# Conditioned decoder layer, one core: modulation two channel blocks ahead, first weight block earlier in two queues, remainders first in each VectorE step

## What is computed

```python
c_act = jax.nn.silu(c)
mod = (c_act @ w_ada[l] + b_ada[l])[:, None, :]
sh1, sc1, g1, sh2, sc2, g2 = jnp.split(mod, N_MOD, axis=-1)
h = rmsnorm(x, norm1_g[l]) * (1 + sc1) + sh1
z = h @ w_in                      # then split into u, gb, gc, v, ga, gg
...                               # pooling, short conv, Conformer conv -> y
x = x + g1 * y
h = rmsnorm(x, norm2_g[l]) * (1 + sc2) + sh2
x = x + g2 * (jnp.square(jax.nn.relu(h @ w_ff1[l])) @ w_ff2[l])
```

## Time and profile before

| | us |
|---|---|
| median of 3 runs | 1137.24 (1134.82 to 1137.81) |
| the profiled execution, its own time | 1136.67 |
| its span, first to last instruction | 1134.8 |
| busy in the span: PE, DVE, ACT, POOL | 1096.7, 596.2, 285.0, 299.9 |
| chain that ended last, by engine | PE 80%, DVE 15%, all else 5% |
| granted clock of TensorE, mean | 0.985 |

### The profile page before, as it was taken

One profiled execution on the slowest core, in us unless ns is written; L12 is line 12 of the kernel. 1 busy time (PEld: TensorE's weight loads), 2 busy tenths in 40 slices (PEclk: granted clock), 3 DMA queues, 4 the chain that ended last, 5 costly groups with the idle time before them and its releaser, 6 DMA issues.

```text
span 1134.8 us, 16579 instructions
## 1 busy us (share of the span) xinstructions
PE 1096.7 (97%) x6979; PEld 1067.4 (94%) x6979; DVE 596.2 (53%) x734; ACT 285.0 (25%) x301; POOL 299.9 (26%) x303
## 2 busy tenths in 40 slices
PE   6899999997999999999999999999999999999996
PEld 5688889997899899999999999999999999999996
DVE  5897789999478454423423332433342342323355
ACT  6321121111145244311401320321330240232111
POOL 2742224333136322121212121222212121213200
PEclk8899999999899999999999999999999999999999
DMA  9978211101012111111111111111111111111212
GB/s 280 342 276 310 61 38 38 56 24 46 25 46 60 30 56 48 46 41 53 39 55 39 56 38 56 38 56 39 57 38 49 45 47 47 43 51 40 72 51 100
DMA packets 97174, 83.17 MB, mean 73 GB/s; under 512 B 2663, under 2 KB 92718, under 8 KB 95039
## 3 DMA queue, kind: packets, MB, share of 16 engines
q1 hardware_dynamic: 96685, 80.97, 22.4%
q0 software_dynamic: 336, 0.58, 0.2%
q10 hardware_dynamic: 82, 0.55, 0.2%
HBM read 77.77 MB, written 4.81 MB: 73 GB/s over the span
## 4 chain that ended last, share of the span: by engine, by line
PE 80%; DVE 15%; SPq 2%; issue 2%; DMA 1%; ACT 0%; DVEq 0%; ACTq 0%
PE acc L1320 69%; DVE dc L956 7%; PE acc L1341 3%; SPq L361 1%; PE modps L1455 1%; PE acc L1616 1%; PE acc L1614 1%; PE acc L1615 1%; DVE work L975 1%; DVE hlo L1035 1%; DVE work L1105 1%; PE acc L1643 1%; DVE work L1045 1%; PE modps L1433 1%; DVE work L1263 1%
## 5 line engine op out<-in xcount | busy, mean ns | idle before, releaser
L495 POOL TENSOR_TENSOR wlo<-wraw,whi 128x512 fp32r<-128x512 f32 (+2 forms) x89 | 117.6, 1322 | 744.2 <-ACT whi L596 744.2
L596 ACT ACTIVATE whi<-wraw 128x1024 fp32r<-128x1024 f32 (+2 forms) x89 | 91.0, 1023 | 669.3 <-PE acc L1320 634.5
L1320 PE MATMUL acc<-hhi,whi 128*128 128x348 f32 (+1 forms) x1080 | 231.1, 322 | 2.7 <-issue 2.2
L1320 PE MATMUL acc<-hhi,wlo 128*128 128x348 f32 (+1 forms) x1080 | 230.2, 321 | 0.0
L1320 PE MATMUL acc<-hlo,whi 128*128 128x348 f32 (+1 forms) x1080 | 229.6, 321 | 0.0
L1320 PEld LDWEIGHTS acc<-hhi,whi 128*128 128x128 f32 x1080 | 181.6, 188 | 7.5 <-issue 7.1
L1320 PEld LDWEIGHTS acc<-hlo,whi 128*128 128x128 f32 x1080 | 182.0, 188 | 0.0
L1320 PEld LDWEIGHTS acc<-hhi,wlo 128*128 128x128 f32 x1080 | 181.8, 188 | 0.0
L1012 DVE SCALAR_TENSOR_TENSOR xT<-acc,modT,xT 128x688 f32<-128x688 f32 x64 | 59.7, 933 | 222.9 <-PE acc L1320 222.9
L1320 PE MATMUL acc<-hid_lo,whi 128*128 128x344 f32 x672 | 142.5, 320 | 0.0
L1320 PE MATMUL acc<-hid_hi,whi 128*128 128x344 f32 x672 | 142.4, 320 | 0.0
(11 more groups left out here) (201 smaller groups left out, 1100.8 us busy)
## 6 DMA issues: line engine op xcount, KB each, us to landing
wraw<-in_w_ff SPq DMA_DIRECT2D x64, 512.0 KB, 3.7
ada<-in_w_ada SPq DMA_DIRECT2D x16, 1024.0 KB, 8.3
wraw<-in_w_in SPq DMA_DIRECT2D x17, 512.0 KB, 4.4
ada<-in_w_ada SPq DMA_DIRECT2D x16, 512.0 KB, 6.7
xrow<-in_x_prompt SPq DMA_DIRECT2D x8, 512.0 KB, 8.2
out<-work SPq DMA_DIRECT2D x6, 512.0 KB
wraw<-in_w_out SPq DMA_DIRECT2D x8, 320.0 KB, 3.2
wraw<-in_w_out SPq DMA_DIRECT2D x4, 384.0 KB, 3.1
```

The costliest lines, as they stand in the source:

```text
L495: nc.gpsimd.tensor_tensor(o[:, 0:cut], a[:, 0:cut], b[:, 0:cut], ALU.subtract)
L596: nc.scalar.activation(whi[:, slot, 0:n, :].rearrange("p k n -> p (k n)"), wraw[:, slot, 0:n * P], ACT.Copy).then_inc(whi_ready, 1)
L1320: last = nc.tensor.matmul(out[:, t, 0:tw], w[:, slot, b, :], x[:, k, t * tw:(t + 1) * tw], start=(i == 0 and w is whi and x is hi), stop=( ...
```

## The change

Four places change. `COLS_AHEAD` goes from 3 to 2, so that TensorE takes up block k of unit 0 one step sooner, right behind M(k+2) in place of M(k+3). In SP's queue the load of weight unit 0 moves from behind the second modulation block to ahead of it. On ScalarE the rounding of unit 0 moves ahead of the three copies of the inverse roots. On VectorE `h_low(step-2)` moves from the end of its step to the head.

```diff
-COLS_AHEAD = 3
+COLS_AHEAD = 2
...
             load_ada(0)
+            load_w(0)
             load_ada(1)
-            load_w(0)
...
+            high_of(0)
             spread_copy(1, CHUNK_AT["norm1"])
-            high_of(0)
             h_high()
...
             for step in range(KD + 2):
+                if step >= 2:
+                    h_low(step - 2, 0)
                 if step < KD:
                     cols_to_rows(step)
                 if 1 <= step <= KD:
...
                     h_pre(step - 1, A1)
-                if step >= 2:
-                    h_low(step - 2, 0)
```

## The result

Median of the device time over five runs of each kernel, taken on the same chip:

| | before | after |
|---|---|---|
| median | 1134.82 us | 1141.71 us |
| lowest to highest | 1133.49 to 1137.81 | 1140.27 to 1142.44 |
| profiled execution (span) | 1136.67 (1134.8) | 1142.44 (1140.6) |
| mean granted clock of that execution | 0.985 | 0.985 |

What follows compares the result with a forecast made beforehand. TensorE bound the stage before; VectorE with ScalarE would after. From h_pre(0) at 31.22, seven 5.02 us steps, the tail and one collision end it at 75.7, 5.6 us later: 1136.67 + 5.6 = 1142.3 us, range 1139.0 to 1145.3.

Steps and rivals of the forecast that it cites:

- part 4: VectorE: h_low directly behind h_pre idles for ScalarE's rounding in each of eight steps, adding 1.36 us; step 5.02 us.
- the sum: h_pre(0) at 31.22, seven steps of 5.02, h_low(7), TensorE's rest and a collision: stage ends at 75.7, 5.6 us later.
- One GpSimd collision: GpSimd's remainder of unit 1 holds up VectorE in the stage: about 0.95 us, taken between 0 and 1.93.
- Part 1: Head, transfer queue: weight unit 0 loaded ahead of modulation block 1 makes M(1) and h_pre(0) 1.18 us later.
- I keep the landing times by place: Head: equal transfers land by queue position, so weight unit 0 at 24.0 us and block 1 complete at 28.9 us.
- Part 2: ScalarE: rounding unit 0 first ends the three copies at about 27.5 in place of 27.14 us, at no cost.
- Part 3: TensorE: unit 0 starts behind M(2), filling waits at the head; a gain taken alone, given no size.
- rival (c): TensorE's clock falls to half again while it waits in steps 2 and 3: at most 2.5 us, 1144.8 us; chance 0.12.
- (a): VectorE's wait for the rounding is hidden and TensorE stays the stage's bound: 2.9 us faster, 1133.8 us; chance 0.10.
- (b): VectorE's wait is there, but the transfer queue and GpSimd's collision cost nothing: 1139.1 us; chance 0.13.
- (d): The stage's delay is absorbed later, by slack between 70 and 287 us: 1136.7 us; chance 0.05.

Runs made afterwards that it cites:

- the unit-0 kernel: Kernel before with only weight unit 0's load moved ahead of modulation block 1 and its rounding ahead of the three copies: 1134.99 us, ratio 0.9998.
- the remainders alone: Kernel before with only h_low moved to the head of its step on VectorE, look-ahead still 3: 1141.96 us, ratio 1.0049; run again, 1140.66 us.

## Why the prediction was right, and where its steps were not

**The deciding step, part 4, held.** `h_low` stands idle 1.28 to 1.29 us in all eight, released by L632, and starts 33.73 - 31.16 = 2.57 us after its `h_pre`, forecast 2.56. The step is 4.94 us where the sum had 5.02 (seven times 0.08, 0.6 us less): the 3.66 us taken for a step before came from two steps, and one of them held an idle gap of 0.28 us, seen in the timeline of VectorE before:

```profile
48.59 1.29 DVE L878 SCALAR_TENSOR_TENSOR work<-xT,A,work 128x1024 f32<-128x1024 f32 x1 [0.28 <-DVE A L903]
```

That the loss comes from here is shown three ways: the edit alone gives it, lengthening the rounding lengthens each step only where the remainder stands at the head, and shortening the round trip gives about half back.

**One GpSimd collision** was taken, 0.95 us; one came, 2.24 - 1.28 = 0.96 us.

**Part 1 had the right size and the wrong cause.** It called M(1) at 28.95 and `h_pre(0)` at 31.22; the profile has 28.89 and 31.16. But the step "I keep the landing times by place" failed. Block 1's second transfer was issued at 20.8 us and landed 6.3 us later, at 27.1, not 28.9. The row, SP's issue in the changed kernel as in the earlier trace rows:

```profile
L361 SPq DMA_DIRECT2D ada<-in_w_ada x1: 1424/1424/1424, 20.8 to 20.8; - x1
...
DMA to landing us min/median/max: 6.3/6.3/6.3
```

M(1) was late because M(0) and the spread sums ahead of it ran at half clock, 1.77 and 2.95 us where full clock takes 1.07 and 2.00. At full clock, in the second profile, the transfer did hold M(1) up, by 0.59 us; with the unit-0 moves alone it did not. So the move cost between 0 and 0.6 us in the four profiles of the new queue order with a head at full clock, not 1.18, and the first profile's agreement was chance. The 28.9 us itself was one profile's: in five others of the old order the fifth transfer landed between 27.2 and 28.0 us.

**Part 2** held: the rounding cost nothing. T(0) was late, at 28.36, by the same half clock; at full clock, in the second profile, it starts at 27.18 us, before 27.24.

**Part 3 said "Taken alone this is a gain".** Taken alone it is the largest loss of all, 21 us. The sentence behind it named the reason, that block k's product wants `hlo(k)` a step sooner, but gave it no price.

**The sum.** Start to end of the stage was forecast as 75.7 - 31.22 = 44.5 us. The profiles of the changed kernel have 45.21 and 44.08. The difference between them is VectorE's wait of 1.02 us for M(5), rival (c) in part: in the first the clock fell to half from 44 to 50 us and came back, at a price of 1.1 us, not 2.5; in the second it was down for a shorter time (0.66 from 44 to 46 us, 0.50 to 48), and no such wait followed. The wait of the first profile was not in the sum, and the steps were too long in it; the two cancel in part. The end came at 76.37 and 74.72, forecast 75.7. The time itself, 1142.3 against 1141.71, agrees in part by its base: it was counted from the profiled 1136.67 us, 1.85 above the median in the result, so a loss of 5.6 us was forecast where the ratio gives 5.8 and the medians 6.9. The clock does not carry the loss: over the chain its mean is 0.89 and 0.92 in the two profiles and 0.87 in the kernel before.

**The other rivals.** (a), the wait hidden, fell: TensorE waits for L632 in the last step as in the first. The Trainium skill's page "VectorE: DVE Perf Modes", section "Rules for kernel authors", advises for chained VectorE operations to minimise their count, not their semaphores. It does not speak of a chain that leaves the engine and comes back, so it does not make a reordering free: here the same count of operations in another order stands idle 10.3 us in eight waits. (b) fell on the size of the collision, not on the queue. (d) fell: 6.27 us at L1455, 6.27 at the pooling mixer, 5.8 in the span. Of the clock, the same skill's page "TensorE: Matmul & The Clock Gate", section "HAM oscillation — how this bites in real kernels", shows bursts that are shorter than the waits for transfers between them and start at half clock each time. Here the clock falls in the wait of 1.86 us ahead of 44.72 us, though that is shorter than the work behind it, but it was back at 1.00 from 52 us on and stayed there through waits of 1.12 and 1.15 us, the last ahead of 70.16 us.

**What the time adds.** The second profile ends the stage 1.65 us sooner than the first and yet took 0.8 us longer as a whole; so a single time measures the stage to no better than about 2 us. By the chain, 45.21 and 44.08 against 40.06 us, the loss is 5.2 and 4.0 us. But 40.06 is one profile: the unit-0 kernel, with VectorE's and TensorE's old order, has 38.63 and 38.46 us, and against these the loss is 5.5 to 6.7 us, about what the times show. Nor does the granted clock of the whole execution explain the times: its mean is 0.9862 over the five of the changed kernel and 0.9855 over the 53 of the kernel before that ran beside the experiments.

## What to carry to other kernels

An operation that consumes another engine's answer to the one just before it, on an engine that works in order, pays that answer's full duration and the hand-over, each time round; put one step of other work between them, and price this before counting what the consumer further on gains. Starting products a step sooner needs slack on the engine that feeds them: here VectorE had 0.75 us a step and the round trip wanted 1.28. When a forecast number agrees with a profile, look whether its cause does too; a second profile of the same program is a cheap way.

## What the runs showed of the hardware that was not expected

TensorE's clock at the head differs between executions of one program. The changed kernel had 0.50 from 24 to 26 us in one profile and 1.00 in the other; the kernel with the remainders alone had 0.50 there in one and 1.00 in the other. `h_pre(0)` starts at 29.0 to 30.6 us where the head ran at full clock, at 31.0 to 33.7 where it did not (in three of these 0.75 us later by GpSimd's remainder), so a difference of 1 to 3 us in one timeline can be this alone. In most profiles the clock fell once from about 14 to 20 us and was back by 22. In the changed kernel's first it fell again near 23 us; in the first of the remainders alone it did not come back before 28 us; in that of the look-ahead alone it stayed at 1.00 until 20 us and fell only then. What decides between these stays open.

Of the transfers: the fifth 512 KB behind x landed at 28.9 us in the one profile of the kernel before. In five other profiles with the same order in the queue it landed at 27.2, 27.3, 27.5, 28.0 and 28.0 us, and in eight with the changed order between 26.9 and 29.4 us (27.1 and 28.3 in the two of the changed kernel). So a landing time read from one profile holds to no better than about 2 us here, and the two orders are not told apart by it. What decides between the executions was not tried.
